# A mixed-attention encoder kernel: row of maxima made and turned a step sooner, outputs turned a step later, VectorE's work between jobs spread anew

## The chip, the cores and the metric

The kernel runs on one core of one Trainium2 chip. The metric is the device time of one execution in microseconds; lower is better. The engines are TensorE (PE in the profile, its weight loads PEld), VectorE (DVE), ScalarE (ACT), GpSimd (POOL) and SyncE (SP, which only issues DMAs here).

## What is computed

Two layers (DEPTH = 2) over a sequence of 1024 tokens of width 1024. In each layer one projection of the stream gives queries, keys and values of four groups of four heads of width 64, and the four kinds of attention go through one output projection, a layer norm, a squared-ReLU MLP of width 4096 and a second layer norm:

```python
proj = einsum('btd,dp->btp', x, w_in[l])
o_a = chunked_relpos_attention(...)        # A: band of 9 chunks of 64 keys, learned bias by distance
o_b = sliding_window_gqa_sinks(...)        # B: window of 2 chunks, a learned sink in each softmax
o_c = differential_attention(...)          # C: two softmax maps a head, p0 - lam * p1, RMS norm
o_d = dsa_attention(...)                   # D: top 256 keys a query by an indexer's score
x = layer_norm(ALPHA * x + einsum('btm,md->btd', concat([o_a, o_b, o_c, o_d]), w_out[l]))
x = layer_norm(ALPHA * x + einsum('btf,fd->btd', square(relu(x @ w_up[l])), w_down[l]))
```

All of it is in float32. The kernel splits operands of the large products in a high and a low part.

## The kernel before

**Stages of a layer.** The input projection with the indexer's scores and the search for each query's 256th largest score; attention; output projection and norm; MLP and norm. Attention is the part that the change touches. It begins at about 291 us in layer 0 and at 1691 us in layer 1.

**Jobs and steps.** Attention is a list of 20 jobs, in the order of heads C, A, B, D (`HEADS`, `JOBS`): a C head makes two jobs (m = 0 and 1, its two maps), so jobs 0 to 7 are C, 8 to 11 A, 12 to 15 B, 16 to 19 D. A job has two halves of 512 queries, and its steps go over tiles of 128 keys: 4 + 8 = 12 steps, 9 for a B job (`STEPS`; `at_step(n)` gives job, step in the job and number of steps). All engines walk the same list of 228 steps, each with its own part of step n:

- TensorE (line 1144 on): `score_t(n)`, the scores with keys in rows (lines 1051; 1055 to 1064); `pv(n - 2)`, the product with the values (1080); `score` pieces (1019 to 1022), which make the **next** job's scores with queries in rows, from which the maxima come; then, where they fall due, `turn_qk` (999), `turn_max` (1029) and `turn_out` (1088).
- ScalarE (1425 on): `exponent(n)` (1414), the high part of a turned pair (1360), `take_max` (1398, 1406), `evacuate` (1422), which copies a finished half out of PSUM three steps after its last key tile.
- VectorE (1834 on): `largest` (1734), the maxima of one piece; `take_lo` (1654), the low part of a turned pair; `take_output` (1762 to 1770), which divides a turned output by its sum; `row_max` (1746, 1747); `between` (1787), work that has nothing to do with the steps and is done once a job.

**The row of maxima.** A job's first `score_t` needs the row of its maxima as one more row of the queries' tile. The chain is: last piece at step total - 5; at step total - 4 VectorE makes the row (`maxima_done_at`, after that step's `take_output`) and goes on with `between`; at step total - 3 TensorE turns it (`max_turn_at`, behind that step's scores and values); ScalarE copies it and issues a DMA that writes the row into the tile; TensorE waits for that DMA (`m_row`) at the next job's first step.

**Bank 4 of PSUM** takes three kinds of small transposes, in one fixed order (`_misc_turns`, `misc_before`): a pair's queries and keys (two heads are a pair, four turns each), the row of maxima, and a finished half's output. A turn into it waits until the one before has been read: pairs by `take_lo` (`qk_lo`), the row by ScalarE (`m_copied`), an output by VectorE (`o_out`). An output is turned `TURN_LAG` = 5 steps after its half's last step: for a job of 12 steps at step 8 (first half) and at step 4 of the next job (second half); in a B job at step 8 and at step 4 of the next. A pair's four turns are placed by `_pair_steps`: from a given step on, at least two steps apart, not in a step that turns a row of maxima, not in one that turns an output, nor in the one before it.

**Work between jobs** (`between`, lines 1787 to 1813), all on VectorE, in order: job 0 compares the scores of three tiles with their thresholds (`above`) and takes the bias of the far keys; jobs 0 and 1 scale the A bias for two heads each (`scale_bias`, line 1703, 256 columns each); job 2 turns the transposed bias (`turn_bias`: four scalings, a high and a low part of 1024 columns); jobs 3, 4, 5, 6, 9, 11 select the 256 keys for one tile of queries each, of 384, 512, 640, 768, 896 and 1024 columns (`select`, lines 1690 to 1698: a comparison, a scan that numbers the ties, three more passes); job 8 squares and sums the C outputs (1775, 1776); job 10 takes their inverse root; jobs 16 and 17 scale them. GpSimd rotates later heads' queries and keys in the first jobs.

**SyncE** copies each head's parts into the tiles for its job (`stack`, 6 or 12 DMAs of 128 or 256 KB), once the pair's low parts are there and the tile's last job has made its scores.

**The end.** In the last job `turn_mix` (1099) turns the attention output for the output projection: transposes 0 to 7 at steps 1 to 8, 8 to 11 at steps 9 to 12 (`mix_turns_at`); the projection (1126) waits until all twelve are split.

## Time and profile before

| | us |
|---|---|
| runs, median of 3 | 2837.42 (2831.07 to 2839.69) |
| the profiled execution, its own time | 2830.91 |
| its span, first to last instruction | 2829.1 |
| attention, layer 0 and layer 1 | 329.2 and 330.9 |

| engine | busy us | share of the span |
|---|---|---|
| TensorE | 2705.2 | 96% |
| VectorE | 1668.2 | 59% |
| POOL | 1285.0 | 45% |
| ScalarE | 977.6 | 35% |

A row of a timeline gives the start in us, the duration, engine, line and operation, and in brackets how long the engine had been idle and what ended that. A row of waits gives who waited for whom, the total, the number and the longest. A matmul's recorded end is modelled, and matmuls overlap; a queue's own work (a DMA's issue) is marked with a q. PEclk is the granted share of TensorE's full clock of 2.4 GHz; 0.50 is 1.2 GHz.

### The profile page before, as it was taken

What the parts mean: (1) busy time and instruction counts of PE and PEld (TensorE: products, weight loads), DVE (VectorE), ACT (ScalarE), POOL (GpSimd) and SP (SyncE); (2) the same over time, 40 slices, a digit from 0 to 9 for tenths busy, and PEclk for the clock granted to TensorE, in tenths of its full rate; (3) what the DMA queues carried; (4) which work ended last, traced back from release to release, by engine and by line L of the source; (5) the groups of instructions that cost most, each with busy time, mean ns of one, the idle gap of its engine ahead of it and who ended that gap; (6) DMA issues with size and microseconds to landing.
All of it is one profiled execution on the core that took longest, in us unless ns stands there. A gap on an engine that the chain in (4) does not pass through costs nothing.

```text
span 2829.1 us, 36218 instructions
## 1 busy us (share of the span) xinstructions
PE 2705.2 (96%) x12768; PEld 2109.7 (75%) x12768; DVE 1668.2 (59%) x3364; ACT 977.6 (35%) x2011; POOL 1285.0 (45%) x1186
## 2 busy tenths in 40 slices
PE   8999889999999999999989998899999999999996
PEld 7788457768788888888777874576787888888885
DVE  3787777545544345534959867765355544445549
ACT  2466444442222212222225654444422222212231
POOL 5433700014666556565554345001156666556562
PEclk9999999999999999999999989999999999999998
DMA  5312234523301111111342132345223101111102
GB/s 152 86 46 59 53 74 96 124 89 119 122 27 39 60 60 60 57 39 33 95 135 54 45 81 46 71 99 127 109 90 112 49 24 48 60 60 60 56 19 100
DMA packets 98570, 207.41 MB, mean 73 GB/s; under 512 B 14138, under 2 KB 23290, under 8 KB 98106
## 3 DMA queue, kind: packets, MB, share of 16 engines
q1 hardware_dynamic: 88952, 177.68, 23.4%
q10 hardware_dynamic: 9440, 27.43, 2.7%
q8 instruction: 103, 1.69, 0.3%
q14 instruction: 75, 0.61, 0.1%
HBM read 142.24 MB, written 8.61 MB: 53 GB/s over the span
## 4 chain that ended last, share of the span: by engine, by line
PE 83%; DVE 12%; DMA 2%; SPq 1%; issue 1%; ACT 1%; POOL 0%; ACTq 0%; DVEq 0%; POOLq 0%
PE ps L1193 8%; PE ps L1195 8%; PE ps L1194 8%; PE ps L1080 7%; PE ps L1218 7%; PE ps L1217 6%; PE ps L1219 6%; PE ps L873 4%; PE ps L875 4%; PE ps L874 4%; PE ps L1128 2%; PE ps L1126 2%; PE ps L1127 2%; DVE x L1882 1%; PE ps L1055 1%; DVE x L1880 1%
## 5 line engine op out<-in xcount | busy, mean ns | idle before, releaser
L829 POOL TENSOR_TENSOR wlo<-wraw,whi 128x512 fp32r<-128x512 f32 (+2 forms) x368 | 492.0, 1337 | 249.7 <-ACT whi L1278 227.8
L827 POOL CAST whi<-wraw 128x512 fp32r<-128x512 f32 (+2 forms) x272 | 180.6, 664 | 743.4 <-DMA wraw<-in_w_out 299.9
L1193 PE MATMUL ps<-xhi,whi 128*128 128x512 f32 x1024 | 406.8, 397 | 3.5 <-DVE xlo L1546 3.5
L1195 PE MATMUL ps<-xhi,wlo 128*128 128x512 f32 x1024 | 406.6, 397 | 0.0
L1194 PE MATMUL ps<-xlo,whi 128*128 128x512 f32 x1024 | 406.4, 397 | 0.0
L1953 DVE TENSOR_TENSOR common<-common,ps 128x512 f32<-128x512 f32 x104 | 69.6, 687 | 460.5 <-PE ps L1219 460.0
L1218 PE MATMUL ps<-wlo,op_hi 128*128 128x512 f32 x784 | 311.7, 398 | 0.0
L1217 PE MATMUL ps<-whi,op_hi 128*128 128x512 f32 x784 | 309.5, 395 | 0.0
L1219 PE MATMUL ps<-whi,op_lo 128*128 128x512 f32 x784 | 308.0, 393 | 0.0
L1414 ACT ACTIVATE probT<-ps 128x512 f32<-128x512 f32 (+2 forms) x456 | 204.8, 456 | 272.4 <-PE ps L1051 108.1
L829 POOL TENSOR_TENSOR wlo<-down_raw,whi 128x512 fp32r<-128x512 f32 x168 | 226.0, 1349 | 98.7 <-ACT whi L1278 91.9
L1080 PE MATMUL ps<-probT,raw 128*65 128x512 f32 (+2 forms) x720 | 266.1, 453 | 0.0
L873 PE MATMUL ps<-whi,xhi 128*128 128x512 f32 (+1 forms) x640 | 246.2, 385 | 7.6 <-DVE xlo L1546 5.1
L1463 ACT ACTIVATE hidden<-ps 128x512 f32<-128x512 f32 x128 | 75.9, 599 | 510.9 <-PE ps L1195 500.1
L1899 DVE TENSOR_TENSOR op_lo<-hidden,op_hi 128x512 fp32r<-128x512 f32 x196 | 203.9, 1085 | 74.6 <-ACT op_hi L1486 69.8
L875 PE MATMUL ps<-whi,xlo 128*128 128x512 f32 (+1 forms) x640 | 242.3, 379 | 0.0
L874 PE MATMUL ps<-wlo,xhi 128*128 128x512 f32 (+1 forms) x640 | 241.8, 378 | 0.0
L1193 PEld LDWEIGHTS ps<-xhi,whi 128*128 128x128 f32 x1024 | 193.2, 189 | 51.0 <-DVE xlo L1546 3.9
L1194 PEld LDWEIGHTS ps<-xlo,whi 128*128 128x128 f32 x1024 | 193.3, 189 | 47.1
L1195 PEld LDWEIGHTS ps<-xhi,wlo 128*128 128x128 f32 x1024 | 193.2, 189 | 47.2
L1953 DVE TENSOR_TENSOR x<-x,ps 128x512 f32<-128x512 f32 x248 | 169.9, 688 | 49.4 <-PE ps L1219 46.2
L1486 ACT ACTIVATE op_hi<-hidden 128x512 fp32r<-128x512 f32 x196 | 111.0, 621 | 247.3 <-PE ps L1219 202.4
(234 smaller groups left out, 5479.7 us busy)
## 6 DMA issues: line engine op xcount, KB each, us to landing
wraw<-in_w_up SPq DMA_DIRECT2D x144, 256.0 KB, 3.1
down_raw<-in_w_down SPq DMA_DIRECT2D x112, 256.0 KB, 3.7
wraw<-in_w_in SPq DMA_DIRECT2D x80, 256.0 KB, 2.7
slot<-q_part SPq DMA_DIRECT2D x72, 256.0 KB
slot<-k_part SPq DMA_DIRECT2D x72, 256.0 KB
wraw<-in_w_out SPq DMA_DIRECT2D x64, 256.0 KB, 2.8
wraw<-in_w_down SPq DMA_DIRECT2D x32, 256.0 KB, 2.6
slot<-q_part SPq DMA_DIRECT2D x48, 128.0 KB
```

The source lines that it names most:

```text
L829: nc.gpsimd.tensor_tensor(wlo[j][:, 0:w], loaded, whi[j][:, 0:w].bitcast(F32), ALU.subtract).then_inc(S["w_lo"], 1)
L873: mm(o, a, whi[j][:, 0:w], start=(k == 0), stop=False)
L874: mm(o, a, wlo[j][:, 0:w], start=False, stop=False)
L875: last = mm(o, b, whi[j][:, 0:w], start=False, stop=(k == KT - 1))
L1080: mm(ps[0:HD + 1, 5 + turn % 2, P * (a - 4 * half):P * (b - 4 * half)], values(kind, h, kt), probT[n % 4][:, 0:P * (b - a)], start=fresh, ...
L1193: mm(ps[:, b, :], wh, xhi[:, k, tok], start=(k == 0), stop=False)
L1194: mm(ps[:, b, :], wh, xlo[:, k, tok], start=False, stop=False)
L1195: last = mm(ps[:, b, :], wl, xhi[:, k, tok], start=False, stop=(k == KT - 1))
L1217: mm(ps[:, bank, :], a, whi[j][:], start=(i == 0 and not more), stop=False, skip_group_check=more)
L1218: mm(ps[:, bank, :], a, wlo[j][:], start=False, stop=False, skip_group_check=more)
L1219: last = mm(ps[:, bank, :], b, whi[j][:], start=False, stop=(i == 1), skip_group_check=more)
L1953: ins = v_.tensor_tensor(xs, xs, p, ALU.add)
```

## The change

Five things are edited. `TURN_LAG` goes from 5 to 6, so outputs are turned a step later: at step 9 of a job of 12 and at step 5 of the next (step 0 and step 5 of the next in B). VectorE makes the row of maxima at step total - 5, right behind the last piece and ahead of `take_lo` and `take_output`; `between` stays at step total - 4, now by itself. TensorE turns the row at the head of step total - 3, ahead of its scores and values, ScalarE takes it ahead of its exponential, and the order in bank 4 follows. The turns of pairs are placed by the same rule, with the new lag: among others pair 1's third turn goes from step 5 to step 6 of job 1, pair 2's fourth from step 5 to 6 of job 5; the fourth turns of pairs 3, 4 and 5 from step 0 of jobs 8, 9 and 11 to step 10 of jobs 7, 8 and 10; pair 7's second from step 5 to step 3 of job 15, its third and fourth from steps 0 and 2 of job 16 to step 7 of job 15 and step 1 of job 16. Transposes 8 to 11 of `turn_mix` go from steps 9 to 12 to steps 10 to 13.

The work between jobs is spread anew: bias scaling in jobs 1 and 4 instead of 0 and 1; the high and low part of the turned bias in job 3 instead of 2; a selection is cut in two, `find` (comparison and scan) and `select` (the other three passes), and the six tiles' finds lie in jobs 4, 5, 6, 7, 9, 13, their selects in jobs 4, 5, 6, 9, 12, 14.

```diff
--- before.py
+++ after.py
@@ -322,7 +322,7 @@
 FIRST_STEP = [min(n for n, z in enumerate(STEPS) if z[0] == j) for j in range(len(JOBS))] + [N_STEPS]
 HALF_END = [n for n, z in enumerate(STEPS) if z[6]]
 HALF_OF = {n: m for m, n in enumerate(HALF_END)}
-LAG, TURN_LAG = 2, 5
+LAG, TURN_LAG = 2, 6
 LAST_STEPS = TURN_LAG + 1
 
 
@@ -360,9 +360,11 @@
 def mix_turns_at(n):
 
     g = n - FIRST_STEP[-2]
-    if 1 <= g <= EARLY:
-        assert g <= TILES or n > HALF_END[2 * len(JOBS) - 2] + TURN_LAG
+    late = HALF_END[2 * len(JOBS) - 2] + TURN_LAG - FIRST_STEP[-2]
+    if 1 <= g <= TILES:
         return [g - 1]
+    if late < g <= late + EARLY - TILES:
+        return [TILES + g - late - 1]
     return []
 
 
@@ -377,6 +379,11 @@
 
 def maxima_done_at(n):
     j, g, total = at_step(n)
+    return 0 < j and j + 1 < len(JOBS) and g == total - 5
+
+
+def between_at(n):
+    j, g, total = at_step(n)
     return j + 1 < len(JOBS) and g == total - 4
 
 
@@ -386,7 +393,9 @@
 
 
 PAIR_AT = {1: (1, 0), 2: (4, 8), 3: (7, 1), 4: (8, 1), 5: (10, 1), 6: (11, 6), 7: (15, 1)}
-SELECT_AT = {3: 0, 4: 1, 5: 2, 6: 3, 9: 4, 11: 5}
+
+FIND_AT = {4: [0], 5: [1], 6: [2], 7: [3], 9: [4], 13: [5]}
+SELECT_AT = {4: [0], 5: [1], 6: [2], 9: [3], 12: [4], 14: [5]}
 PARTS_OF = [0, 0, 0, 0, 1, 0, 1, 0]
 
 
@@ -418,11 +427,11 @@
         yield "qk_lo", 4 * 0 + j
     yield "m_copied", 0
     for n in range(N_STEPS + LAST_STEPS):
+        if max_turn_at(n):
+            yield "m_copied", at_step(n)[0] + 1
         if pair_turn_at(n):
             p, j = pair_turn_at(n)
             yield "qk_lo", 4 * p + j
-        if max_turn_at(n):
-            yield "m_copied", at_step(n)[0] + 1
         if n - TURN_LAG in HALF_OF:
             yield "o_out", HALF_OF[n - TURN_LAG]
 
@@ -1142,6 +1151,8 @@
                 last.then_inc(S["t_ready"], 1)
 
             for n in range(N_STEPS + LAG):
+                if max_turn_at(n):
+                    turn_max(at_step(n)[0] + 1)
                 if n < N_STEPS:
                     score_t(n)
                 if LAG <= n < N_STEPS + LAG:
@@ -1150,8 +1161,6 @@
                     score(at_step(n)[0] + 1, p)
                 if pair_turn_at(n):
                     turn_qk(*pair_turn_at(n))
-                if max_turn_at(n):
-                    turn_max(at_step(n)[0] + 1)
                 if n - TURN_LAG in HALF_OF:
                     turn_out(HALF_OF[n - TURN_LAG])
                 for i in mix_turns_at(n):
@@ -1423,12 +1432,12 @@
 
             take_max(0)
             for n in range(N_STEPS + LAST_STEPS):
+                if max_turn_at(n):
+                    take_max(at_step(n)[0] + 1)
                 if n < N_STEPS:
                     exponent(n)
                 if pair_turn_at(n):
                     take_turn(*pair_turn_at(n))
-                if max_turn_at(n):
-                    take_max(at_step(n)[0] + 1)
                 if n - LAG - 1 in HALF_OF:
                     evacuate(HALF_OF[n - LAG - 1])
                 split_hi(mhi, 16, mix_turns_at(n))
@@ -1683,12 +1692,17 @@
                 for j in part:
                     then(compare(j, thr[:, COL[j]:COL[j] + 1], ALU.is_gt, count2))
 
-            def select(j):
+            def find(j):
 
                 n, c = SEL_N[j], COL[j]
                 eq, run = late1[:, 0:n], late2[:, 0:n]
                 then(v_.tensor_scalar(eq, seg(j), thr[:, c:c + 1], None, ALU.is_equal))
                 then(v_.tensor_tensor_scan(run, eq, eq, 0.0, ALU.add, ALU.max))
+
+            def select(j):
+
+                n, c = SEL_N[j], COL[j]
+                eq, run = late1[:, 0:n], late2[:, 0:n]
                 then(v_.scalar_tensor_tensor(out=eq, in0=run, scalar=count2[:, c:c + 1], in1=eq,
                                              op0=ALU.is_le, op1=ALU.mult))
                 then(v_.scalar_tensor_tensor(out=eq, in0=seg(j), scalar=thr[:, c:c + 1], in1=eq,
@@ -1709,6 +1723,9 @@
                     then(v_.tensor_scalar(bias_raw[:, h], bias_raw[:, h], far[:, h:h + 1], HD ** 0.5,
                                           ALU.subtract, ALU.mult))
                 then(v_.memset(bias_raw[CHUNK:P, :, 0:CHUNK], -float(2 ** 100)))
+
+            def split_bias():
+
                 then(v_.tensor_copy(bias_hi[:], bias_raw[:]))
                 v_.tensor_tensor(bias_lo[:], bias_raw[:], bias_hi[:].bitcast(F32), ALU.subtract
                                  ).then_inc(S["bias_t_ready"], 1)
@@ -1793,16 +1810,22 @@
                     then(v_.tensor_scalar(count2[:], count2[:], -1.0, float(TOPK), ALU.mult, ALU.add))
                     dve.wait_ge(S["bias_loaded"], 16)
                     then(v_.tensor_copy(far[:].unsqueeze(2), bias_a[:, :, 0:1]))
-                if job in (0, 1):
-                    scale_bias(2 * job)
-                    scale_bias(2 * job + 1)
+                if job in (1, 4):
+                    for h in range(2):
+                        scale_bias(h if job == 1 else 2 + h)
                 if job == 2:
                     dve.wait_ge(S["bias_t_loaded"], 16)
                     turn_bias()
+                if job == 3:
+                    split_bias()
                     then(v_.memset(farmask[:], 0.0))
                     then(v_.memset(farmask[CHUNK:P, 0:CHUNK], -BIG))
-                if job in SELECT_AT:
-                    select(SELECT_AT[job])
+                for j in SELECT_AT.get(job, []) if job == 9 else []:
+                    select(j)
+                for j in FIND_AT.get(job, []):
+                    find(j)
+                for j in SELECT_AT.get(job, []) if job != 9 else []:
+                    select(j)
                 if job == 8:
                     square_c(0)
                     square_c(4)
@@ -1834,14 +1857,14 @@
             for n in range(N_STEPS + LAST_STEPS):
                 for p in pieces_at(n):
                     largest(at_step(n)[0] + 1, p)
+                if maxima_done_at(n):
+                    row_max(at_step(n)[0] + 1)
                 if pair_turn_at(n):
                     take_lo(*pair_turn_at(n))
                 if n - TURN_LAG in HALF_OF:
                     take_output(HALF_OF[n - TURN_LAG])
                 split_lo(mlo, mhi, 16, mix_turns_at(n))
-                if maxima_done_at(n):
-                    if at_step(n)[0]:
-                        row_max(at_step(n)[0] + 1)
+                if between_at(n):
                     between(at_step(n)[0])
             dve.wait_ge(S["o_out"], 2 * len(JOBS))
             v_.memset(flip[:], 0).then_inc(S["mix_done"], 1)
```

## Rows read from the trace of the kernel before

**Rows 1.** Page, part 1: busy time, share of the span, instructions.

```profile
PE 2705.2 (96%) x12768; PEld 2109.7 (75%) x12768; DVE 1668.2 (59%) x3364; ACT 977.6 (35%) x2011; POOL 1285.0 (45%) x1186
```

**Rows 2.** Windows: attention of both layers; columns: us, busy of engines (count), PEclk, DMA share, GB/s.

```profile
291.00:620.20 329.20, 305.36 (x1698) 206.53 (x1697) 217.12 (x675) 147.99 (x331) 55.13 (x58) 0.98 0.35 77
1691.00:2021.90 330.90, 305.95 (x1699) 206.01 (x1697) 217.79 (x675) 148.26 (x331) 55.50 (x57) 0.98 0.35 77
```

**Rows 3.** Waits of PE in attention: line, releaser, us in total, times, longest.

```profile
PE ps L1029 <- DVE mr L1747: 11.3, 14, 2.1
PE ps L1051 <- DMA slot<-mT: 8.3, 10, 2.4
PE ps L1019 <- DVE nm L1734: 7.2, 7, 2.3
...
PE ps L999 <- DVE q_part L1654: 6.8, 4, 2.5
PE ps L1088 <- ACT oe L1422: 4.5, 7, 0.7
PE ps L999 <- DVE mix L1767: 4.0, 6, 0.9
```

**Rows 4.** The same, waits of the weight load.

```profile
PEld ps L1029 <- DVE mr L1747: 33.4, 37, 2.6
...
PEld ps L1051 <- DMA slot<-mT: 17.7, 14, 3.0
...
PEld ps L1055 <- DMA slot<-mT: 7.2, 14, 0.7
```

**Rows 5.** Timeline of PE from job 4 to job 5: start us, us, operation.

```profile
364.97 0.27 PE L1029 MATMUL ps<-ident_r,mr 128*8 128x128 f32 x1
...
366.56 0.81 PE L1080 MATMUL ps<-probT,raw 128*65 128x384 f32 x2
367.37 0.50 PE L1051 MATMUL ps<-slot 105*128 105x512 f32 x1
...
369.38 0.66 PE L999 MATMUL ps<-ident_r,raw 128*128 128x128 f32 x4 [0.84 <-DVE q_part L1654]
```

**Rows 6.** Timeline of VectorE, same boundary.

```profile
362.79 0.68 DVE L1734 CUSTOM_DVE_ANT_0 junk<-ps,zero 128x512 f32<-128x512 f32 x1
...
363.99 0.18 DVE L1762 RECIPROCAL rinv<-ps 128x4 f32<-128x4 f32 x1 [0.51 <-PE ps L1088]
...
364.74 0.17 DVE L1747 TENSOR_SCALAR mr<-nm 128x8 fp32r<-128x8 f32 x1
...
365.33 1.23 DVE L1691 TENSOR_TENSOR_SCAN late<-late 128x512 f32<-128x512 f32 x1
...
368.17 0.43 DVE L1698 TENSOR_SCALAR selmask<-late 128x512 bf16<-128x512 f32 x1
```

**Rows 7.** Timeline of ScalarE, same boundary.

```profile
365.28 0.27 ACT L1398 ACTIVATE mT<-ps 8x128 fp32r<-8x128 f32 x1 [0.56 <-PE ps L1029]
365.57 0.63 ACTq L1406 DMA_DIRECT2D slot<-mT  x1
```

**Rows 8.** Windows: behind a wait of job 1, layer 1; and ahead of job 6.

```profile
1709.90:1713.10 3.20, 3.20 (x9) 1.92 (x8) 1.79 (x7) 1.84 (x4) 3.02 (x3) 0.50 0.00 0
...
382.00:388.00 6.00, 3.10 (x13) 1.70 (x14) 4.69 (x9) 1.42 (x4) 0.94 (x1) 1.00 1.00 214
```

**Rows 9.** Timeline of VectorE at the end of job 8: first and last of the squares.

```profile
434.89 1.22 DVE L1775 TENSOR_TENSOR squares<-mix 128x1024 f32<-128x1024 f32 x1
...
438.66 1.22 DVE L1776 TENSOR_REDUCE ms<-squares 128x16 f32<-128x1024 f32 x1
```

**Rows 10.** Source view of line 1703: duration ns min/median/max, first and last start.

```profile
L1703 DVE TENSOR_SCALAR bias_a<-bias_a,far x8: 282/786/1256, 305.3 to 1721.9; 128x256 f32<-128x256 f32 x8
```

**Rows 11.** Timeline of PE, pair's turn at the start of job 12.

```profile
495.27 1.12 PE L999 MATMUL ps<-ident_r,raw_d 128*128 128x128 f32 x4 [2.54 <-DVE q_part L1654]
```

**Rows 12.** Timeline of PE, start of the output projection.

```profile
620.27 0.50 PE L1126 MATMUL ps<-whi,mhi 128*128 128x512 f32 x1 [1.19 <-DVE mlo L1546]
```

## The prediction

> **What bounds the kernel now.** I read the page first: TensorE is busy for 2705.2 us, 96% of the span [rows 1], so only what TensorE loses counts. The edits touch only the attention stretch of each layer, so the second view is the windows of those two: 329.2 and 330.9 us, with TensorE idle for 23.8 and 25.0 us and VectorE busy for only two thirds [rows 2]. VectorE has room; what is late is the order of its work. The third view is who TensorE waits for. Rows 3 take a wait only where the modelled end of the matmul before is past, rows 4 count the weight load's wait, which begins while TensorE still streams. The loss lies between: in [rows 5] the first score of job 5 starts the moment the modelled end before it is reached, no idle time shown, and still ends 0.50 us after it, where 512 columns at 2.4 GHz are 0.21 and back-to-back passes end 0.23 apart. I read losses as such distances from end to end, beyond a pass's own streaming; they come to about 44 us a layer.
>
> One boundary shows the pattern [rows 5 to 7]. VectorE ends the last piece of the next job's maxima at 363.47, waits for the turned output, takes it from 363.99 (0.65 us), and only then makes the row, ready at 364.91. TensorE turns it at 364.97, ScalarE copies it at 365.28 and issues its DMA at 365.57, and the next job's first score starts at 367.37: 2.40 us behind the turn, about 1.80 of them DMA. Behind the row VectorE does a selection until 368.60, and a turn of queries waits for it until 369.38, 0.84 us.
>
> **The sum, both layers together.**
>
> 1. *The wait for maxima* (line 1029). Bounds 11.3 and 33.4 us [rows 3, 4]; nearest the first, as most of the second is streaming: 12.8. After the change the row is made 0.35 us after the last piece, without the output turn. TensorE, asking a step sooner (a C step is 0.23 of score and 2 x 0.43 of values, read between ends: 1.09), asks about when it is ready; I leave 0.2 at five boundaries a layer. The share in B and in job 15 is priced below. Gain 6.7.
>
> 2. *The wait for the row's DMA*. Bounds 8.3 in 10 waits [rows 3] and 24.9 (17.7 and 7.2) [rows 4]. Ten waits with 0.25 hidden in each and some fourteen like that of rows 5 (0.27) make 14.4. In the step that now lies behind the turn are a score (0.17), values (0.86) and the output's four transposes (0.24), 1.27 us more cover; a boundary needs 2.40 and gets 3.4. All go but job 6's: there the row is 3.0 us late [rows 4], because SyncE's copies of the next pair saturate the DMA engines (share 1.00) [rows 8]. It is issued some 2 us sooner against them, as its pair moves a step back: about 1.0 a layer is left. Gain 12.3. The DMA issue holds ScalarE's queue for 0.63 us [rows 7] ahead of that step's exponential, which TensorE needs two steps later, after some 1.9 us: no cost.
>
> 3. *Pieces held by a late VectorE* (line 1019, 7.2 in 7 waits at least [rows 3]; 11.6 from end to end with line 1021). These follow job 0's comparisons and bias scaling, job 2's bias turn and the selections of jobs 6 and 9. The comparisons no longer wait for an output turn and start while VectorE is idle; the scaling leaves job 0, where one took up to 1256 ns against 282 at best [rows 10]; the bias split goes to job 3. All move about a step earlier, since the output's taking now comes behind them. I keep 0.6 at job 7. Gain 11.6 less that, 10.4.
>
> 4. *Turns of queries and keys* (line 999). Waits of 10.8 us at least [rows 3]; end to end 14.5 to be removed, among them the largest, 2.5 idle and 2.9 in all behind the 1024-column selection of job 11 [rows 11], which is split over jobs 13 and 14. But here is what the change adds. An output turned in a job's step 9 is taken by VectorE **behind** the job's selection, and bank 4 of PSUM is free only then. A pair's turn in step 10 waits for both. Its distance from TensorE's turn of maxima is 2.4 us in C (two steps and the transposes), 2.9 in A. Job 4: two scalings (0.9 with their memsets, at the 282 ns of [rows 10] and a little over) and a 384-column search and selection, about 3.1 by the 512-column one of 3.7 [rows 6], then the output, 0.65: 4.7 against 2.4, a wait of 2.3. Job 8: the squares take 4.99 us [rows 9], the output 0.65, begun 0.4 before TensorE's turn: 2.6. Job 7: a 768-column search, 2.5 (half as much again as the 512-column one, 364.91 to the end of its scan at 366.56 [rows 6]), and an output of 0.9: 1.0. Job 10: 0.3; job 1: 0.1. New cost 6.3 a layer, 12.6. Net 1.9.
>
> 5. *B jobs* (12 to 14). With nine steps the second output's turn now comes at step 5, and the maxima's at the head of step 6 waits for bank 4: the output's taking stands in its way, 0.65 to 0.85 us. The wait for ScalarE's copy, 4.5 us in 7 [rows 3], goes, but it lay beside the row's DMA, which had to be waited for anyway, and a turn of 0.24 comes out of that shadow. Minus 0.5 at three boundaries a layer: minus 3.0.
>
> 6. *Job 15*: the pair's second turn moves two steps ahead of the maxima and the output behind them. The row comes some 1.4 us sooner. Gain 3.0. Selections in B: about 3.2 us each beside 3.9 us in which VectorE is free; nothing.
>
> 7. *The clock.* After four of the long waits the granted clock is 0.50 for over 3 us, as in [rows 8]: 2.4 GHz falls to 1.2, about 1.6 us lost each. Two of the four follow waits that go in part 3, one that of [rows 11]. The new waits of 2.3 and 2.6 us, twice each, are as long; I count three such stretches. Gain 2.
>
> 8. *The end.* The late mix turns move by a step, so the last is turned behind the last values, and the wait before the output projection (1.19) [rows 12] grows by 0.2 a layer: minus 0.4.
>
> Sum 6.7 + 12.3 + 10.4 + 1.9 - 3.0 + 3.0 + 2 - 0.4 = 32.9. A TensorE that comes sooner meets VectorE and ScalarE less far along; I take off 2 for that, and forecast **31 us**. The profiled execution took 2830.91, so it would take 2800; the median shown is 6.5 higher, 2837.42, and the forecast for it is **2806**. What follows attention is fed by it and bound by TensorE, so the gain passes on whole.
>
> The Trainium skill has a rule that bears on part 7: TensorE: Matmul & The Clock Gate, section Loop structure matters more than you think, says that copying results out by VectorE between dense matmul groups does not make TensorE go cold, and blames waits on DMA. Here the trace differs: the stretch in rows 8 follows a wait for VectorE. By the page the new waits would cost only their own length, and the sum would be about 5 us better.
>
> **The rivals.**
>
> *The new waits take half of it* (0.25). The work between jobs stands in front of the output in most of them; if each of the six long new waits (jobs 4, 7, 8, twice) costs a half-rate stretch (10 us instead of 5) and the bank makes a wait of 1 us at five more places a layer, 15 us are lost of 31: 2821. For it: VectorE is in order, and nothing else can free bank 4. Against: only six jobs have a pair's turn in step 10.
>
> *Slower* (0.05). The turn of maxima now stands at the head of its step, before a score and a value product, which before went first. If VectorE ends the last piece more than a step behind TensorE, every boundary pays. Thirty-eight boundaries must lose over 0.85 us each to use up 33; at 1.4, two pieces behind, it is 20 us slower: 2857. Against it: in [rows 6] the last piece was done at 363.47 and TensorE would ask at about 363.7.
>
> *No change* (0.08): the waits end last at something else. If ScalarE's exponentials, now behind the row's issue, hold the next step by what the row gains (about 0.8 at each boundary), the time stays within 0.3%, 8.5 us, which is what a measurement here can tell from nothing.
>
> *The forecast* has 0.62.
>
> The range holds, below, all new waits at no more than half and no half-rate stretch, 13 us better: 2793. Above it takes in the first rival with 4 us for its unknowns: 2825. Chances: faster 0.87 (forecast and first rival), same 0.08, slower 0.05.
>
> **What would show it.** In the profile after: line 1029 waiting for the row of maxima near zero outside B, with about 0.8 there against the output (line 1767); the first scores waiting for the row's DMA only in job 6; line 1019 nearly without waits for VectorE; line 999 waiting for the output's taking in jobs 4 and 8, 2.3 and 2.6 us, and no longer in job 12. Idle of TensorE in the two stretches down from 49 to some 25 us. The forecast is wrong if line 1029 still waits in C jobs, or if line 999's waits exceed 20 us.

## The result and the profile after

The changed kernel takes **2804.49 us** (median of 4 runs, 2802.57 to 2810.08) against 2836.36 (4 runs, 2831.07 to 2839.69): ratio 0.9899, 95% interval 0.9881 to 0.9916. Forecast were 2806 and a gain of 31. The profiled execution, 2810.08 with a span of 2808.3, is its slowest run: against the profiled 2830.91 of before it shows a gain of 20.8, not 31. So the forecast total came out in the medians, and the profiled pair alone does not bear it out; the rest of this document is about where the sum was wrong and what made it up.

Page of the changed kernel, part 1:

```profile
PE 2697.7 (96%) x12768; PEld 2111.0 (75%) x12768; DVE 1670.5 (59%) x3364; ACT 976.7 (35%) x2011; POOL 1283.9 (46%) x1186
```

Windows of its two attention stretches, columns as in [rows 2]:

```profile
289.90:609.20 319.30, 300.71 (x1700) 205.73 (x1699) 218.18 (x675) 147.61 (x331) 55.29 (x58) 0.99 0.36 80
1679.80:2001.30 321.50, 303.62 (x1699) 207.71 (x1699) 218.14 (x675) 147.65 (x331) 55.27 (x56) 0.98 0.36 79
```

The same instructions as in [rows 2], 9.9 and 9.4 us shorter. TensorE's idle time in the two windows is 18.6 + 17.9 = 36.5 us; it was 48.8, and about 25 was forecast. By the prediction's own sign ("wrong if line 1029 still waits in C jobs") its part 1 fails here: that turn still waits in C jobs, 1.07 us idle at most. Its waits from the first attention to the end of the second (line numbers of TensorE and ScalarE are 9 higher than before; 1751, 1764 and 1784 of VectorE were 1734, 1747 and 1767):

```profile
PE ps L1038 <- DVE mix L1784: 8.8, 8, 1.6
PE ps L1008 <- DVE mix L1784: 8.6, 4, 2.4
PE ps L1038 <- DVE mr L1764: 7.4, 14, 1.3
...
PE ps L1060 <- DMA slot<-mT: 4.8, 3, 2.1
...
PE ps L1008 <- DVE other L1784: 1.3, 2, 0.7
PE ps L1064 <- ACT probT L1423: 1.1, 6, 0.2
```

Held against [rows 3]: the wait of the first scores for the row's DMA fell from 8.3 in 10 waits to 4.8 in 3, pieces (lines 1019 and 1021 before) have all but gone, and the turn of the maxima (1029 before, 1038 now) rose from 11.3 to 7.4 + 8.8. Losses read from end to end, as the prediction did, summed over both layers of the two profiled executions:

| loss, us | before | after | gain | forecast |
|---|---|---|---|---|
| turn of maxima outside B, for the row (part 1) | 9.2 | 9.9 | -0.7 | 6.7 |
| row's DMA (part 2) | 14.8 | 6.2 | 8.6 | 12.3 |
| pieces (part 3) | 12.9 | 0.5 | 12.4 | 10.4 |
| turns of pairs outside job 15 (part 4) | 15.7 | 12.5 | 3.2 | 1.9 |
| B jobs and job 15, all but the DMA (parts 5, 6) | 12.9 | 14.6 | -1.6 | 0.0 |
| half-rate passes, the end and all else (parts 7, 8, margin) | | | -1.1 | -0.4 |

The gains add to 20.8; the last line's forecast is 2, -0.4 and the 2 taken off. One boundary, that from job 4 to job 5, shows what the change does. TensorE of the changed kernel, as [rows 5]:

```profile
355.64 0.27 PE L1038 MATMUL ps<-ident_r,mr 128*8 128x128 f32 x1 [0.23 <-DVE mr L1764]
...
360.12 0.66 PE L1008 MATMUL ps<-ident_r,raw 128*128 128x128 f32 x4 [1.89 <-DVE mix L1784]
```

VectorE, as [rows 6]:

```profile
354.49 0.69 DVE L1751 CUSTOM_DVE_ANT_0 junk<-ps,zero 128x512 f32<-128x512 f32 x1
...
355.41 0.17 DVE L1764 TENSOR_SCALAR mr<-nm 128x8 fp32r<-128x8 f32 x1
355.49 0.35 DVE L1717 TENSOR_SCALAR bias_a<-bias_a,far 128x256 f32<-128x256 f32 x1
...
359.02 0.36 DVE L1712 TENSOR_SCALAR selmask<-late 128x384 bf16<-128x384 f32 x1
...
359.64 0.42 DVE L1784 TENSOR_TENSOR mix<-ps,rinv 128x256 f32<-128x256 f32 x1
```

The row is ready 0.40 us behind the last piece (in [rows 6] it was 1.44), and TensorE, which asks a step sooner, waits 0.23 for it (0.40 from end to end); before, it did not wait at this boundary. In jobs 3, 5 and 7 the same turn did wait, and there the change helps. TensorE in job 3, before and after (no idle time of note is left):

```profile
351.38 0.27 PE L1029 MATMUL ps<-ident_r,mr 128*8 128x128 f32 x1 [0.77 <-DVE mr L1747]
342.46 0.27 PE L1038 MATMUL ps<-ident_r,mr 128*8 128x128 f32 x1
```

Back to job 4. Behind the row VectorE works from 355.49 to 359.38 before it takes the output, and the pair's turn needs that output's bank: 1.89 us idle, 2.11 from end to end, where 2.3 was forecast.

### The profile page after: what moved, and what is told of

Its sections match the earlier page's. It is cut to its first block, busy times and chain, and to the rows that moved or that the text cites. A ratio compares the mean times of both kernels' runs of the same rounds, so it can differ in the third digit from the quotient of the medians.

```text
span 2808.3 us, 36228 instructions
## 1 busy us (share of the span) xinstructions
PE 2697.7 (96%) x12768; PEld 2111.0 (75%) x12768; DVE 1670.5 (59%) x3364; ACT 976.7 (35%) x2011; POOL 1283.9 (46%) x1186
## 4 chain that ended last, share of the span: by engine, by line
PE 84%; DVE 10%; DMA 2%; issue 1%; SPq 1%; ACT 1%; ACTq 0%; POOL 0%; DVEq 0%
PE ps L1202 8%; PE ps L1203 8%; PE ps L1204 8%; PE ps L1089 8%; PE ps L1227 7%; PE ps L1226 7%; PE ps L1228 6%; PE ps L882 4%; PE ps L884 4%; PE ps L883 4%; PE ps L1137 2%; PE ps L1135 2%; PE ps L1136 2%; DVE x L1905 1%; PE ps L1031 1%
```

## Experiments

The last column is the mean over the runs of span times granted clock: roughly the span that a kernel would have with TensorE at its full clock (it counts half of every half-rate stretch as lost to the clock, also where TensorE waits in it). The clock is recorded to 0.001, so a single value is good to 1.4 us.

| kernel | median, runs | ratio, 95% interval | mean clock | span x clock |
|---|---|---|---|---|
| before (beside the first four) | 2835.58, 11 | | 0.9817 | 2780.7 |
| the change, again | 2807.60, 4 | 0.9907, 0.9892 to 0.9921 | 0.9830 | 2758.4 |
| e1 order alone | 2823.12, 6 | 0.9954, 0.9940 to 0.9968 | 0.9812 | 2767.7 |
| e2 spread alone | 2812.69, 5 | 0.9921, 0.9909 to 0.9933 | 0.9836 | 2764.0 |
| e3 work behind output | 2801.01, 4 | 0.9881, 0.9868 to 0.9894 | 0.9840 | 2754.1 |
| e4 pair 2 in job 5 | 2804.66, 4 | 0.9896, 0.9881 to 0.9911 | 0.9842 | 2759.7 |
| e5 B outputs sooner | 2810.80, 4 | 0.9909, 0.9895 to 0.9924 | 0.9818 | 2756.4 |
| e6 = e3 + e5 | 2802.20, 4 | 0.9881, 0.9864 to 0.9897 | 0.9835 | 2754.2 |
| e7 = e6, exponentials first in B | 2804.45, 4 | 0.9891, 0.9876 to 0.9906 | 0.9835 | 2756.2 |
| e8 B outputs later, on e3 | 2801.78, 4 | 0.9888, 0.9873 to 0.9902 | 0.9845 | 2756.0 |
| e9 = e8, pair 2 in job 5 | 2798.45, 4 | 0.9881, 0.9864 to 0.9897 | 0.9855 | 2756.4 |
| e10 = e3 + e4 | **2797.54**, 4 | 0.9869, 0.9853 to 0.9886 | 0.9852 | 2754.7 |
| e11 without GpSimd's turns | 2805.37, 4 | 0.9899, 0.9884 to 0.9914 | 0.9825 | 2755.0 |

The runs fall in four groups, each with runs of the kernel before beside it, and the ratios are taken within a group: e0 (the change again) to e3; e4 to e7 (before 2835.06, last column 2782.0); e8 and e9 (2833.28, 2780.4); e10 and e11 (2834.35, 2781.3). So the last column of one and the same kernel moves by up to 1.6 us from group to group, and smaller differences between groups mean nothing. "Against the changed kernel" below is against its repeat, 2807.60 and 2758.4.

**The change again**, for the spread of its own runs.

> The changed kernel as it is. In the two profiled executions TensorE's losses in attention, read from end to end, fall from 44.1 and 45.6 us to 33.5 and 35.7, 20.5 us in all, and the spans differ by 20.8 us, while the medians shown differ by 31.9. Theory A (the sum's 31 us is real, and the two profiled executions differ in half-rate stretches of the clock by chance): the medians differ by 29 to 33 us again, and before runs at a lower mean clock than this kernel by about 0.3 points. Theory B (20 us is the gain, and the first medians were luck): 19 to 25 us, and no difference of the clock.

28.0 us by the medians, 26.4 by the means: short of the first theory's range, above the second's. The last column parts them: 22.3 us of it are waits and work, and the rest is clock. Of the four runs of the changed kernel behind the result, span times clock is 2757.7 to 2759.3 for all, while their times run from 2802.57 to 2810.08: what differs among executions is how much of the time TensorE ran at half rate. The profiled pair set one of the shorter runs of before against the longest of after.

**e1, the order alone**: every edit to the order of the steps, with the old work between the jobs.

```
-LAG, TURN_LAG = 2, 5
+LAG, TURN_LAG = 2, 6
...
-SELECT_AT = {3: 0, 4: 1, 5: 2, 6: 3, 9: 4, 11: 5}
+FIND_AT = {3: [0], 4: [1], 5: [2], 6: [3], 9: [4], 11: [5]}
+SELECT_AT = {3: [0], 4: [1], 5: [2], 6: [3], 9: [4], 11: [5]}
```

> Order alone: the row of maxima sooner and the outputs later, with the work between jobs lying as before. By my working: the waits for the row and its DMA go as in the changed kernel; the long waits for bank 4 stay or grow, above all at the pair's turn of job 11, behind the 1024-column selection and the output: 6.5 + 0.65 less the 2.9 of cover, about 3.9 us a layer; job 3's first pieces wait about 1.5 us behind the whole bias turn. Gain of 10 to 14 us against before (ratio 0.995 to 0.9965). Rival (the sooner row is the whole of the gain, the spread hides nothing that was in the way): within 4 us of the changed kernel.

12.5 us, as expected. Waits of TensorE in its second attention stretch:

```profile
PE ps L1008 <- DVE mix L1784: 8.1, 3, 3.9
...
PE ps L1028 <- DVE nm L1751: 2.2, 1, 2.2
```

The 3.9 is job 11's pair turn behind the output behind the whole 1024-column selection, 4.2 from end to end, where 3.9 was expected. The old order had a wait behind the same selection too, 2.9 and 2.8 at the start of job 12; the new order alone makes it longer, and the spread takes it away. The 2.2 is job 3's first piece behind the whole bias turn, where 1.5 was expected.

**e2, the spread alone**: the old order with the new placing of bias work and selections.

```
+FIND_AT = {4: [0], 5: [1], 6: [2], 7: [3], 9: [4], 13: [5]}
+SELECT_AT = {4: [0], 5: [1], 6: [2], 9: [3], 12: [4], 14: [5]}
```

> Spread alone: the work between jobs as in the changed kernel, with rows and outputs at their old steps. By my working: the 2.9 us at the start of job 12, the waits of pieces in jobs 1 and 3 (1.8 and 2.3 us) and part of those in jobs 7 and 10 go, and with them three or four half-rate stretches of 1.6 us; line 1029's waits and those for the row's DMA stay. Gain of 17 to 21 us against before (ratio 0.9925 to 0.994). Rival (the spread only pays once the row is sooner): under 8 us.

22.9 by the medians, slightly above, and 16.7 by the last column: the waits at the start of job 12 (2.91 and 2.77 from end to end before) are gone, and no wait for a piece in attention is over 0.6. The two halves give 12.5 and 22.9 alone and 28.0 together (13.0, 16.7 and 22.3 by the last column). Part of the overlap can be seen: the waits for job 1's pieces, 1.50 and 1.44 from end to end before, are gone with either half alone. The rest is not taken apart.

**e3, the work between the jobs behind the output** where a pair's turn or heavy work follows:

```
-    return j + 1 < len(JOBS) and g == total - 4
+    return j + 1 < len(JOBS) and g == total - (3 if j in (4, 7, 8, 10) else 4)
```

> The changed kernel with the work between jobs one step later, behind the output's taking, in jobs 4, 7, 8 and 10. Theory A (the long waits at the pair's turn in step 10 come from the amount of VectorE's work there, and the order only moves them): the waits of line 999 at jobs 4 and 8 (2.1 and 2.6 us) go from step 10, but 2.5 us come back at the next pair's turn in job 5 and about 2 us at the first pieces of job 9; jobs 7 and 10 gain 0.9 and 0.3. In all 1 to 4 us faster than the changed kernel. Theory B (it is the order alone): all four waits go and nothing comes back: 6 us a layer and half-rate stretches, 14 us faster than the changed kernel.

6.6 us faster than the changed kernel. Its waits in the first attention stretch:

```profile
PE ps L1008 <- DVE q_part L1663: 2.2, 1, 2.2
PE ps L1060 <- DMA slot<-mT: 2.1, 1, 2.1
PE ps L1030 <- DVE nm L1751: 1.4, 2, 1.1
```

No pair's turn waits for an output any more; the turn of the maxima in B still does (4.4 us in 4 waits). But job 4's 2.11 us came back as 2.41 at the pair's next turn, behind the same VectorE work, and job 8's 2.63 as 1.38 at the first maxima of job 9; those of jobs 7 (0.88) and 10 (0.30) went whole. By its end-to-end losses that is 2.1 us a layer, 4.3 by the last column. The waits behind the output are the change's own cost, 12.5 us in both layers, and a third of them came only from the order of VectorE's work.

**e4, pair 2 turned in job 5.**

```
-PAIR_AT = {1: (1, 0), 2: (4, 8), ...
+PAIR_AT = {1: (1, 0), 2: (5, 0), ...
```

> The changed kernel with one thing altered: the four turns of pair 2 start in job 5 (steps 60, 62, 66, 70) instead of at step 8 of job 4 (56, 58, 61, 65). Two things are asked of it. Theory A (the pair turn behind job 4's selections waits 2.1 us for bank 4 because VectorE has its work between the jobs ahead of the output that the turn needs; and the row of job 6 is late by 2.1 to 2.4 us because SyncE's copies of pairs 1 and 2 into the stacks hold all DMA engines, share 1.00, while the row's few bytes go): the wait of 2.1 us at step 58 goes; the row's wait at the head of job 6 goes with the copies, and comes back smaller at the head of job 7 (1.0 in one layer of the changed kernel), whose stretch the copies of pair 2 now fall in: job 7's row waits 2 to 3 us. Net per layer: -2.1 -2.2 +1.5 = -2.8, in all about -5 us. Theory B (the row of job 6 is late because ScalarE's own queue issues it late, or VectorE's maxima are late, and the copies don't matter): the wait at the head of job 6 stays at 2.1 to 2.4 us, the head of job 7 stays at 0 to 1.0, and only the 2.1 of step 58 goes: -4 us in all. The times hardly part the two (the clock alone moves a run by up to 5 us); the waits in the profile at the heads of jobs 6 and 7 do.

2.9 us by the medians, nothing by the last column. The waits say more. In the changed kernel the stretch ahead of job 6 is, in the view of windows:

```profile
374.90:379.40 4.50, 2.64 (x13) 1.09 (x11) 4.25 (x8) 1.06 (x3) 0.94 (x1) 1.00 1.00 231
```

DMA share 1.00 while the row's 4 KB wait. The row was ready in time there (its turn waited 0.10) and its DMA was issued at 374.83; the score that needs it starts at 379.39. With pair 2 in job 5 the stretches ahead of job 6 and of job 7:

```profile
370.00:375.00 5.00, 2.96 (x17) 1.56 (x15) 4.11 (x8) 1.13 (x3) 0.21 (x1) 1.00 0.00 1
385.60:389.70 4.10, 3.44 (x15) 1.52 (x14) 3.93 (x6) 1.30 (x4) 0.00 (x0) 1.00 0.95 227
```

The wait at the head of job 6 is gone in both layers, and job 7's is 0.93 and 1.14: the row is late where SyncE's copies fill the DMA engines, which is theory A, though it is cheaper there than the 2 to 3 expected. A new 2.3 us stands at step 70 behind job 5's own selection, and that is why the time hardly moved.

**e5, B outputs a step sooner.**

```
+OUT_AT = {n + TURN_LAG - (m in (23, 25, 27)): m for m, n in enumerate(HALF_END)}
...
-                if n - TURN_LAG in HALF_OF:
-                    turn_out(HALF_OF[n - TURN_LAG])
+                if n in OUT_AT:
+                    turn_out(OUT_AT[n])
```

> The changed kernel with the outputs of the three sliding-window jobs that end in steps 152, 161 and 170 turned as before, one step sooner than the changed kernel has them (their first halves: turns 23, 25 and 27), so that VectorE takes them from bank 4 a step before the turn of the maxima wants that bank. In the changed kernel the turn of the maxima waits 0.98, 1.18 and 1.18 us there for VectorE's output, and two steps later TensorE waits 0.38 and 0.42 us at each of these boundaries for ScalarE's exponentials, which stand behind the issue of the row's DMA (0.63 us of ScalarE's queue). Theory A (the bank is what the turn of the maxima waits for, and ScalarE's issue what the exponentials wait for, both apart from each other): 1.1 us per boundary go, the 0.8 behind ScalarE stay: -3.3 us per layer, in all -5 to -7 us. Theory B (the wait moves on: with the bank free, the maxima themselves are late at these boundaries, as they are in the first jobs, or the output's turn now waits for ScalarE's copy of the halves as in the kernel before, 0.86 us at each boundary): no more than -1 us in all.

Nothing that can be measured: 3.2 us slower by the medians, 2.0 faster by the last column. The waits fell by 0.12 to 0.15 each. In the changed kernel VectorE did this at the boundary into job 13:

```profile
490.91 0.17 DVE L1764 TENSOR_SCALAR mr<-nm 128x8 fp32r<-128x8 f32 x1
491.05 0.18 DVE L1779 RECIPROCAL rinv<-ps 128x4 f32<-128x4 f32 x1
491.26 0.42 DVE L1784 TENSOR_TENSOR mix<-ps,rinv 128x256 f32<-128x256 f32 x1
```

and in e5 this:

```profile
485.72 0.17 DVE L1765 TENSOR_SCALAR mr<-nm 128x8 fp32r<-128x8 f32 x1
485.80 0.17 DVE L1780 RECIPROCAL rinv<-ps 128x4 f32<-128x4 f32 x1
486.00 0.42 DVE L1785 TENSOR_TENSOR mix<-ps,rinv 128x256 f32<-128x256 f32 x1
```

The row, then at once the output, whichever step the output belongs to. (The lines of e5 to e9 are numbered one or more further than those of the changed kernel.) With its turn a step sooner the output still stands behind the row in VectorE's order, and the turn of the maxima waits for both.

**e6, e3 and e5 together.**

> The changed kernel with two edits together: VectorE's work between the jobs behind the output in jobs 4, 7, 8 and 10 (alone it took 6.6 us off the changed kernel), and the three outputs of the sliding-window jobs turned one step sooner. If the two gains lie at different places, as their waits say, they add up: 2801.0 less what the outputs give alone. Theory A: 2795 to 2796. Theory B (the outputs give nothing): 2800 to 2801.

2802.20: a little above theory B's range and nearer to it than to A's; the last column agrees with e3's within its error.

**e7, exponentials ahead of the row's copy and issue in B**, on e6:

```
-                if max_turn_at(n):
+                if max_turn_at(n) and at_step(n)[0] < 12:
                     take_max(at_step(n)[0] + 1)
                 if n < N_STEPS:
                     exponent(n)
+                if max_turn_at(n) and at_step(n)[0] >= 12:
+                    take_max(at_step(n)[0] + 1)
```

> The kernel with both edits, and in the sliding-window jobs alone ScalarE does the exponentials of the step ahead of taking the turned maxima and issuing the row's DMA, as in the kernel before. Theory A (TensorE's 0.38 and 0.42 us at each of these boundaries stand behind the 0.63 us that ScalarE's queue is held by the issue): they go, and the row lands 0.5 to 0.7 us later, which it can afford now that the turn of the maxima no longer waits: -0.8 x 3 x 2 = -4 to -5 us against the kernel with both edits. Theory B (the row is on the path already: it lands as the next job's first scores want it): the wait only changes its name, from ScalarE's exponentials to the row's DMA, and the time is the same within 1.5 us. Then the price of the issue on ScalarE's queue can't be had back by order alone.

2.3 us slower than e6 (2.0 by the last column, whose single values in e7 spread over 8); no gain, in any case. What the issue held up before, two waits of 0.38 and 0.42, is now one of 1.06 to 1.11 from end to end:

```profile
491.28 0.39 PE L1065 MATMUL ps<-slot 128*128 128x256 f32 x1 [0.79 <-ACT probT L1424]
```

Neither theory had this form in jobs 12 to 14: the wait is still ScalarE's and not the row's. ScalarE's queue is held for 0.63 us by the issue in either order, the exponentials behind it are only others. At the head of job 16 theory B does hold: the first scores wait for the row's DMA, 0.63 from end to end in both layers. This order does not win the price back.

**e8, B outputs behind the turn of the maxima**, on e3: `OUT_AT` with `+ (m in (23, 25, 27, 29))`, and jobs 12 to 15 among those whose work stands behind the output.

> The kernel with VectorE's work between the jobs behind the output (jobs 4, 7, 8, 10, and here 12 to 15 too), and the four outputs that fall in the step ahead of the turn of the maxima in the sliding-window jobs turned one step later, behind that turn, instead of one sooner. One step sooner took away 0.12 to 0.15 us of 0.98 to 1.18 per boundary: VectorE does the last maxima, their last operation and the output in one row, whichever step the output belongs to, and TensorE waits for the end of it. Theory A (what TensorE waits for is the output's two to three VectorE operations, 0.6 to 0.9 us, behind the finished maxima; their being late is the rest): with the output behind the turn, 0.6, 0.8, 0.8 and 0.75 us go, 0.3 stay at each: -3 us per layer, -6 in all against the kernel with both edits (2802.2), and the row goes out sooner by as much. Theory B (VectorE as a whole is what these short jobs of 9 steps wait for: it only shifts its lateness): the wait comes back as scores that wait for maxima (the two next steps) or for bank 4 at the first pair turn of job 15, and no more than 2 us are won.

The turns' waits fell as theory A has it, from 0.98, 1.18, 1.18 and 1.70 in e3 to 0.54, 0.50, 0.49 and 1.12, and 2801.78 shows that nothing was won. ScalarE and VectorE at the boundary out of job 13 tell where it went:

```profile
497.12 0.27 ACT L1408 ACTIVATE mT<-ps 8x128 fp32r<-8x128 f32 x1 [0.44 <-PE ps L1039]
498.87 0.30 ACT L1412 ACTIVATE es<-mr,sinks 128x8 f32<-128x8 f32 x1 [1.48 <-DVE mix L1785]
498.88 0.66 ACTq L1416 DMA_DIRECT2D slot<-mT  x1
```

ScalarE's exponential of the sinks writes a buffer that the last output of two jobs back still reads. With that output later, ScalarE waits 1.48 us for it, ahead of the row's issue, and TensorE 1.5 for ScalarE (in jobs 13 and 14). A dependence that neither theory had counted.

**e9 and e10, pair 2 moved and the work behind the output together**, e9 on e8 and e10 on e3 (job 5 for job 4 in the list).

> The last kernel with pair 2 turned in job 5 (steps 60, 62, 66, 70) and job 5 in place of job 4 among those whose VectorE work stands behind the output. Alone, the move of pair 2 took the waits at step 58 (2.1 us) and at the head of job 6 (2.1 to 2.4) away, and brought 0.5 at step 60, 2.3 at step 70 behind job 5's own selections, and 0.9 to 1.1 at the head of job 7. Theory A (both new ones are VectorE's work ahead of an output, mended as in the other jobs): step 70's wait falls below 0.5; against the last kernel: step 60's 2.4 and job 6's 2.1 go, 1.0 at job 7 and 0.5 at step 60 come: -3 us per layer, about -6 in all. Theory B (the four turns of a pair are late wherever VectorE has 3 to 4 us of other work in the same job): 1.5 to 2.5 us stay at one of the turns in job 5, and -2 us in all or less is won.

> The changed kernel with pair 2 turned in job 5 and VectorE's work between the jobs behind the output in jobs 5, 7, 8 and 10, and the sliding-window jobs left as they are in the changed kernel. Moving outputs there, a step sooner or later, won nothing: later, it took 0.5 us off each turn of the maxima and gave back 0.6 to 1.5 at three places. Theory A (the parts are apart: this is the last kernel without its losses in the sliding-window jobs, 1.5 to 2 us per layer): 2795 to 2797. Theory B (what is won there comes back as the row's wait at the head of job 7 and behind it): no faster than the kernel with the work behind the output alone, 2801.

e9: 3.3 us better than e8 by the medians (the intervals overlap), none by the last column; step 70's wait is gone, as theory A has it, and 1.7 of it is back at a piece in job 6 and 1.5 to 2.5 at the row of job 7. e10: **2797.54, the lowest median here** (e9's is 0.9 above it, which is nothing), 0.9869 (0.9853 to 0.9886) of the kernel before, where the changed kernel has 0.9899 and, in its repeat, 0.9907. Theory A's 2795 to 2797 is missed by half a microsecond, theory B's 2801 by more. Its waits in the first attention stretch:

```profile
PE ps L1038 <- DVE mix L1784: 4.4, 4, 1.5
PE ps L1038 <- DVE mr L1764: 3.0, 7, 1.0
PE ps L1060 <- DMA slot<-mT: 1.6, 1, 1.6
PE ps L1028 <- DVE nm L1751: 1.4, 1, 1.4
```

The last column puts it level with e3 (2754.7 and 2754.1), though, and the intervals of the two overlap: what it has over e3 is clock, 0.9852 against 0.9840. In its profiled run attention has no half-rate stretch left, where that of the changed kernel has four. (Not counted, here and below: TensorE is at half rate when attention begins, for the first 6 us or so, in every profiled run.)

**e11, GpSimd idle beside jobs 1 to 3.** The changed kernel without two of GpSimd's rotations, so it leaves out part of the computation:

```
-                turn(block(B_K, P), 2, cs64, HD // 2, 0, TILES)
...
-                for t0 in range(0, TILES, 2):
-                    turn(raw_d[:, t0:t0 + 2, 0:5 * HD], 5, cs64, HD // 2, t0, 2)
```

> The changed kernel without GpSimd's rotations of the sliding-window jobs' keys and of the last jobs' queries and keys, which run beside jobs 1 to 3 (this leaves part of the computation out: those heads are computed from unrotated parts). In the changed kernel the turn of the maxima still waits 0.8 to 1.2 us in jobs 1 and 2, where 0.2 was foretold. Theory A (VectorE's short operations between SBUF tiles are held until GpSimd's running instruction ends: the one that makes the row takes 1147 ns in job 1, from 313.52 to 314.67, with a GpSimd instruction ending at 314.64, and 171 to 172 where GpSimd is idle): the longest of these 40 operations falls to under 200 ns beside attention, and the two waits fall to 0.3 or 0.4 each: -1.7 per layer, -3 to -5 in all. Theory B (VectorE is late there because it has a pair's turns, or an output of four operations, in front of the last maxima, and GpSimd's part is chance): the waits stay over 0.8 and the time within 1.5 us of the changed kernel.

The waits of job 1 (1.23 and 0.82) are below 0.35, those of job 2 (1.22 twice) are 0.37 both, some 3 us gone. The turn in job 2, in the changed kernel and in e11:

```profile
329.39 0.27 PE L1038 MATMUL ps<-ident_r,mr 128*8 128x128 f32 x1 [1.06 <-DVE mr L1764]
324.39 0.27 PE L1035 MATMUL ps<-ident_r,mr 128*8 128x128 f32 x1 [0.20 <-DVE mr L1761]
```

Ahead of it three short VectorE operations took 0.62, 0.61 and 0.44 us beside GpSimd, and take 0.23, 0.42 and 0.16 without: 0.86 us in all, which is what the wait lost (1.06 to 0.20). In time it is 2.2 us by the medians and 3.4 by the last column, beside the 3 to 5 expected; the repeat of the changed kernel, against which this is, had shorter waits in jobs 1 and 2 (2.7 us idle in its profiled run, 3.8 in the first), so the size of this loss varies from one execution to the next. In jobs 1 to 5 of both layers the operation that makes the row takes 0.17 us each time. The expectation that none of the 40 stays over 0.2 beside attention was missed by three: 1.18 at 288.42, 0.12 us behind the start of a rotation that stayed, and 0.53 and 0.50 in job 17, where GpSimd splits weights.

## Why the prediction was right, and where its sum was not

**Part 1 failed.** "I leave 0.2 at five boundaries a layer": 20 waits of 9.9 us stand there, and the gain of 6.7 did not come. By jobs, from end to end, both layers:

| turn of the row of maxima in | before | after |
|---|---|---|
| jobs 3, 5, 7 | 5.6 | 1.0 |
| jobs 1, 2 | 2.9 | 4.5 |
| jobs 4, 6, 8, 10, 11 | 0.3 | 3.8 |
| job 17 | 0.4 | 0.5 |

Jobs 1, 2, 3, 5 and 7 have the five boundaries that waited before (9.2 less the 2.0 would be 7.2; how much of its 12.8 the sum put into B and job 15 it does not show). In jobs 3, 5 and 7 the step held: the row was ready 2.4 us or more behind the last piece and is now ready 0.40 behind it, and a wait of 0.93 became one of 0.26 or none. It failed in jobs 1 and 2, where VectorE's short operations are held by GpSimd, which e11 shows (some 3 us), and in five jobs where nothing had waited and the sum has nothing: there the row was in time for the old question and is late for the sooner one, by 0.28 to 0.43, as at 355.64. In job 4 the change moved the question by a step of 1.09 us and the answer by 1.04 (1.44 to 0.40 behind the last piece): the two cancel at this line, and what is won is won behind it, at the DMA. I had looked only at boundaries that waited before, without setting the sooner question against the answer at all the others.

**Part 2**: right in kind; a gain of 8.6 against 12.3. I put 1.0 a layer at job 6; it is 2.1 to 2.4. Issued sooner, the row still falls among copies that fill the DMA engines, and e4 shows that these are the cause. Of what else is left, 0.7 stands at the head of job 14 in layer 1 and 1.0 at the head of job 7 in layer 0. At the latter the DMA engines are nearly idle (share 0.04 from 389.90 to 394.00), so it is not the copies. Queues from 390.90 to 392.50, packets, MB, share:

```profile
q8 instruction: 1, 0.02, 5.1%
q10 hardware_dynamic: 16, 0.00, 1.5%
```

The second line is the row; the last of its eight pieces went 0.9 us behind the others. The first is one transfer of 16 KB that ran at the same time. The last section has how often the two are found together. "No cost" for ScalarE's issue was wrong in B: with steps of under 1 us the exponentials behind it are wanted sooner, 0.8 a boundary (0.38 and 0.42 from end to end). It is the mechanism of the rival called no change, at three boundaries a layer.

**Part 3**: right and a little small; 0.5 left of 12.9.

**Part 4**: the best of the steps. Forecast 2.3, 2.6, 1.0 and 0.3 for jobs 4, 8, 7 and 10; measured from end to end 2.11, 2.63, 0.89 and 0.30. A wait put together from the durations of what stands ahead of an instruction, against the distance to it, is good to 0.2 us.

**Parts 5 and 6**: 0.98 to 1.18 at the turn and 0.8 behind ScalarE in B, and 1.7 in job 15. Together a loss of 1.6 where I had 0. Read apart, jobs 12 to 14 lose about 3.5 where I had 3.0, and job 15 gains under 2 where I had 3.0: its turn of the maxima, which waited 1.08 us idle for the row, waits 1.56 for the output.

**Part 7**: half-rate stretches in attention: four before, three forecast, four in the profiled run after and four in the next, at partly other places. This is one of them, behind the wait of job 4 in layer 1 (view of windows):

```profile
1749.70:1753.00 3.30, 3.30 (x12) 2.22 (x11) 1.15 (x4) 1.36 (x3) 0.00 (x0) 0.55 0.00 0
```

As in the stretch of [rows 8] the wait ahead is one for VectorE, so this trace does not agree with the rule weighed in the prediction, that of the Trainium skill (TensorE: Matmul & The Clock Gate, section Loop structure matters more than you think). A count from one profile is one draw, however: the same wait of job 8, 2.63 in both layers, is followed by half rate in one and not in the other.

**Part 8**: 1.41 for 1.19 before the output projection, as forecast.

Without the margin the forecast was 33, the profiled pair gave 21, for which the maxima's turn is 7 short, the row's DMA 4, parts 5 and 6 together nearly 2 and parts 7 and 8 with all else nearly 3, while pieces and turns of pairs came out 3 better. The median still came out at 2804 because the executions behind it run at a higher mean clock than before's, 0.982 to 0.985 against 0.980 to 0.983 (in the 11 runs of before in the table; of before's own runs behind the result only the profiled one's is known), which the profiled pair does not show. By the last column that is worth 4 us in the repeat (26.4 less 22.3), and more in the runs behind the result (31.9 against 23.3 of the profiled pair, 2829.1 x 0.983 less 2808.3 x 0.982), and I had priced it at 2. That the higher clock comes of the shorter waits is likely (both go together in e10) and not shown. So the right total is in part luck: waits and work gave 22 us where the sum had 29 (31 less the 2 for the clock), the clock gave 4 or more where it had 2, and these runs of the change came out 3 us lower than its repeat.

The rival "the new waits take half of it" did not come: the waits at jobs 4, 8, 7 and 10 are as long as the sum had them, 12.5 us in all, and of six no more than three are followed by half rate. Nor did the slower one: the turn of the maxima pays 0.26 to 0.43 at most boundaries, under the 0.85 from which it would decide; it pays more than that only in jobs 1 and 2 and in 12 to 15.

## What to carry to other kernels

When an in-order engine has several clients, set the moment at which each is asked against the moment at which it answers, at every boundary and not only at those that wait now: moving both by a step wins nothing at that line, and can bring a wait where there was none. Of work that is put ahead of something, add up what stands before it and compare it with the distance; this gave four new waits to 0.2 us before anything ran. And compare kernels by span times granted clock besides the median: here it says that of the 28.0 us between two medians 22.3 are waits and work. It has an error of its own, though, 1 to 2 us for a mean of four.

## What the runs showed of the hardware

**A short VectorE operation can last as long as a GpSimd instruction.** VectorE in job 1 of the changed kernel:

```profile
313.32 0.16 DVE L1763 TENSOR_TENSOR nm<-nm 128x4 f32<-128x4 f32 x1
313.52 1.15 DVE L1764 TENSOR_SCALAR mr<-nm 128x8 fp32r<-128x8 f32 x1
```

GpSimd beside it:

```profile
313.46 1.18 POOL L779 TENSOR_TENSOR raw<-raw,turn 128x512 f32<-128x512 f32 x1
```

And the operation over the whole changed kernel (source view; ns, shortest, median, longest):

```profile
L1764 DVE TENSOR_SCALAR mr<-nm x40: 171/172/1147, 281.3 to 1974.6; 128x8 fp32r<-128x8 f32 x40
```

It starts 0.06 us behind GpSimd's instruction and ends 0.03 behind it, where it takes 0.17 alone. The same row's TENSOR_TENSOR 0.2 us earlier, begun before that instruction, is not held; in job 2 such ones take 0.44 and 0.61 in place of 0.16 and 0.42. The operations that read PSUM are the same beside GpSimd and without it, 0.69 for 512 columns. This agrees with the Trainium skill, SBUF — State Buffer, section Who interferes with whom: VectorE and GpSimd share a pair of ports, an instruction that takes it keeps it to its end, and tensor_scalar from SBUF is among those that can want it. e11 shows what it costs this kernel.

**Half-rate stretches come behind waits of TensorE, and not behind each.** The eight in attention of the two profiled executions, before and after, all begin during a wait of 1.1 to 2.5 us idle or less than 2 us behind its end; the wait of 2.4 in job 8 of layer 0, after, has none. Past its first microseconds, attention's stretches at a granted clock of 0.50 last 3.4 us in most places (about twice that in two of e1 and one of e4). They differ from one execution of a kernel to the next, while span times clock of one kernel's runs stays within 2 us (the change's first four) to 8 (e7's four).

**The row's 4 KB are late among large copies, and now and then beside one transfer of another queue.** From the start of its issue to the start of its last piece of 512 bytes the row takes 1.33 to 1.45 us in 31 of the changed kernel's 40 cases, with the DMA engines at a share under 0.2. Ahead of job 6, with the share at 0.98 and 0.99, it takes 3.83 and 3.60. And one takes 2.22 at a share of 0.06, the one at the head of job 7 in layer 0: a transfer of 16 KB on the queue named instruction began at 391.11, before the row's pieces, and took 1.29; seven pieces went at 391.44 to 391.50, the eighth at 392.38. Over the 14 profiled executions here five rows take 2.17 to 2.36 at a share of 0.06 or less, and each has such a transfer inside; other rows have one and are not late. That the eighth piece stood behind the transfer on one DMA engine is inferred from these times.
